# A hybrid block in float32: memory keys and values and the SSD half of the output projection between the stick-breaking heads, SSD products in runs, first stage in another order

## The reference

```python
proj = rmsnorm(h, norm_mix_g) @ w_in          # z, xbc, dt, q, k, v
xbc = silu(causal_dwconv(xbc, conv_w, conv_b))
y = ssd_chunked(xh, dt, a, bm, cm)            # 8 heads of 64, 4 chunks of 128 tokens
y_ssd = rmsnorm((y + d_skip * xh) * silu(z), ssd_norm_g)
# stick-breaking attention, 8 heads of 64: A[t,s] = sigmoid(z_ts) * prod_{s<j<t} (1 - sigmoid(z_tj)), s < t
y_sb = rmsnorm(stick_breaking_attention(q, k, v), sb_norm_g)
h = h + concat(y_ssd, y_sb) @ w_out
m = rmsnorm(mem, norm_mem_g)                  # 256 memory tokens
k = m @ w_xk; v = m @ w_xv                    # 4 heads of 128
q = rmsnorm(h, norm_xa_g) @ w_xq
h = h + softmax(q k^T / sqrt(128)) v @ w_xo
```

## Time and profile before

| | |
|---|---|
| time, median of 3 runs | 2195.87 us (2185.97 to 2202.16) |
| the profiled execution's own time | 2196.22 us |
| its span, first to last instruction | 2194.4 us |
| TensorE busy | 2087.9 us, 95% of the span |
| VectorE, ScalarE, GpSimd busy | 1061.4, 749.7, 229.7 us |
| mean granted TensorE clock | 0.96 |

### The profile page before, as it was taken

One profiled execution on the slowest core, in us unless ns is written; L12 is line 12 of the kernel. 1 busy time (PEld: TensorE's weight loads), 2 busy tenths in 40 slices (PEclk: granted clock), 3 DMA queues, 4 the chain that ended last, 5 costly groups with the idle time before them and its releaser, 6 DMA issues.

```text
span 2194.4 us, 28790 instructions
## 1 busy us (share of the span) xinstructions
PE 2087.9 (95%) x11578; PEld 1763.2 (80%) x11578; DVE 1061.4 (48%) x1429; ACT 749.7 (34%) x975; POOL 229.7 (10%) x198
## 2 busy tenths in 40 slices
PE   7998988999999999999899999999998899999997
PEld 5776656768888888898899999999886578888885
DVE  5654547454444454313244343435598634443434
ACT  4435653353223243331332222123434433222122
POOL 2001022020000022002320000002035210000001
PEclk9997789999999999899899999999999899999998
DMA  4213112212222222111122222222222022222221
GB/s 165 81 74 48 21 39 77 96 58 96 96 96 93 90 86 97 55 61 39 39 90 84 96 94 79 96 96 96 77 77 72 7 77 96 96 96 96 96 84 69
DMA packets 27792, 174.68 MB, mean 80 GB/s; under 512 B 4385, under 2 KB 4513, under 8 KB 7730
## 3 DMA queue, kind: packets, MB, share of 16 engines
q1 hardware_dynamic: 25680, 167.32, 21.5%
q0 software_dynamic: 1856, 5.90, 1.7%
q10 hardware_dynamic: 162, 0.10, 0.0%
HBM read 168.53 MB, written 4.78 MB: 79 GB/s over the span
## 4 chain that ended last, share of the span: by engine, by line
PE 69%; issue 18%; DVE 7%; ACT 4%; POOL 1%; DMA 0%; DVEq 0%; POOLq 0%; ACTq 0%
PE lin L425 56%; PE aux L1959 1%; ACT w_hi L359 1%; PE lin L1140 1%; DVE w_lo L366 1%; PE lin L1150 1%; PE aux L1528 1%; PE aux L1542 1%; POOL squares L601 1%; PE lin L1929 1%; PE aux L1943 1%; PE aux L1119 1%; PE aux L1120 1%; PE aux L1955 0%; PE aux L1556 0%
## 5 line engine op out<-in xcount | busy, mean ns | idle before, releaser
L425 PE MATMUL lin<-v_hi,w_hi 128*128 128x264 f32 (+1 forms) x1712 | 573.7, 335 | 4.8 <-DVE v_lo L586 3.4
L425 PE MATMUL lin<-v_hi,w_lo 128*128 128x264 f32 (+1 forms) x1712 | 571.1, 334 | 0.0
L425 PE MATMUL lin<-v_lo,w_hi 128*128 128x264 f32 (+1 forms) x1712 | 569.5, 333 | 0.0
L425 PE MATMUL lin<-x_hi,w_hi 128*128 128x512 f32 (+1 forms) x1224 | 436.2, 356 | 29.2 <-DMA cst<-in_consts 13.4
L425 PE MATMUL lin<-x_hi,w_lo 128*128 128x512 f32 (+1 forms) x1224 | 433.0, 354 | 0.0
L425 PE MATMUL lin<-x_lo,w_hi 128*128 128x512 f32 (+1 forms) x1224 | 432.6, 353 | 0.0
L366 DVE TENSOR_TENSOR w_lo<-w_raw,w_hi 128x2048 fp32r<-128x2048 f32 (+1 forms) x144 | 328.7, 2282 | 195.9 <-ACT w_hi L359 195.8
L359 ACT ACTIVATE w_hi<-w_raw 128x2048 fp32r<-128x2048 f32 (+1 forms) x155 | 292.9, 1890 | 289.9 <-PE lin L425 285.4
L425 PEld LDWEIGHTS lin<-v_hi,w_hi 128*128 128x128 f32 x1712 | 324.5, 190 | 39.6 <-DVE v_lo L586 3.8
L425 PEld LDWEIGHTS lin<-v_lo,w_hi 128*128 128x128 f32 x1712 | 324.4, 189 | 33.7 <-issue 0.7
L425 PEld LDWEIGHTS lin<-v_hi,w_lo 128*128 128x128 f32 x1712 | 324.3, 189 | 32.1
(11 more groups left out here) (341 smaller groups left out, 2358.9 us busy)
## 6 DMA issues: line engine op xcount, KB each, us to landing
w_raw<-in_weights SPq DMA_DIRECT2D x155, 1024.0 KB, 4.8
rel_by_distance<-rel_vec POOLq DMA_DIRECT2D x1, 2620.0 KB, 56.0
rel_bias<-rel_by_distance POOLq DMA_DIRECT2D x8, 264.0 KB, 3.0
h<-in_x_t SPq DMA_DIRECT2D x4, 512.0 KB, 8.2
out_t<-h SPq DMA_DIRECT2D x4, 512.0 KB, 2.8
mem_in<-in_mem_t POOLq DMA_DIRECT2D x1, 1024.0 KB, 5.1
cst<-in_consts SPq DMA_DIRECT2D x1, 512.0 KB, 9.8
col<-in_cols ACTq DMA_DIRECT2D x1, 67.0 KB, 6.0
```

The source lines that it names most:

```text
L425: last = nc.tensor.matmul(o, a, b, start=(k % (L.kc // k_banks) == 0 and p == 0), stop=((k + 1) % (L.kc // k_banks) == 0 and p == 2))
```

## The change

- **Order of units**: after V come xk, xv, then w_out in two halves, `w_out_a` (the SSD rows) and `w_out_b` (the stick-breaking rows), 2 units each, then xq. xk, xv and w_out_a no longer go through `pe_linear` and its slots.
- **Heads**: TensorE runs two **fills** in each head, one between the logits of the next head and the exponents, one after the values: in heads 0 and 1 the memory keys, in 2 and 3 the memory values, in 4 to 7 two output tiles of w_out_a each; the SSD norm's sums follow head 2. They go to two banks, `fill_banks`; ScalarE or VectorE empties them. The third bank of the exponents moves to `aux[:, 2, 256:512]`, beside the logits' third bank: the logits of head hd therefore wait for `w_att` of head hd - 2, ScalarE makes a copy `z_relu` of this bank's logits, and VectorE reads that.
- **Splits**: ScalarE makes w_hi of six units in the heads, GpSimd makes their w_lo (`pool_stick`), with the squares of the two mixer norms between them.
- **Head 0 earlier**: its logits, hi and lo parts and log terms stand in V; so do the sums and root of the memory norm, whose squares stand in K. The memory is loaded after the convolution's sums. Its operands lie in x_hi[4:8] and x_lo[4:8], its scale by token in `scale_tok[:, 1]`.
- **Bias table**: its columns are copied at the start, its write to DRAM starts when q and k are scaled.
- **SSD products**: `pe_ssd_back` issues the eight seg products in a row, then the eight state products; that of chunk 3 comes after V's second tile instead of the fourth.
- **First unit**: no wait for the constants, both output tiles at once in three passes (w_hi x_hi, w_lo x_hi, w_hi x_lo), with the semaphores of x_hi and x_lo; ScalarE's squares of the first norm come behind the split of unit 1, and VectorE adds them (`dve_squares`).
- **After the heads**: only w_out_b's 8 tiles (12 matmuls each), the root of `l_sb`, then xq.

The diff, cut to its core (buffer places and copied or deleted lines of the old order are left out):

```diff
...
-    ("w_out", 4, 8, 2, S1, False),
-    ("xk", 2, 8, 2, MEM, False), ("xv", 2, 8, 2, MEM, True), ("xq", 2, 8, 2, S1, False),
+    ("xk", 2, 8, 0, MEM, False), ("xv", 2, 8, 0, MEM, True), ("w_out_a", 2, 4, 0, S1, False),
+    ("w_out_b", 2, 4, 4, S1, False), ("xq", 2, 8, 2, S1, False),
...
+        def pe_first_unit(pe, L, hi, lo, N):
+            w = [t[:, 0, :].rearrange("p (k n) -> p k n", k=L.kc) for t in (w_hi, w_lo)]
+            pe.wait_ge(sem("w_hi_ready"), 1)
+            for p, (wp, xp_) in enumerate(((w[0], hi), (w[1], hi), (w[0], lo))):
+                if p == 1:
+                    pe.wait_ge(sem("w_lo_ready"), 1)
+                for m in range(L.tpu):
+                    for k in range(L.kc):
+                        if p == 0 and m == 0:
+                            pe.wait_ge(sem("operand_hi"), N.tiles0 + k + 1)
+                        elif p == 2 and m == 0:
+                            N.wait_operand(pe, k)
...
             act_evacuate(act, XBC, ...
-                after={(1, 1): lambda: act_root(act, l_mix)})
+                after={(0, 0): all_squares, (1, 1): lambda: act_root(act, l_mix)})
...
             next_lo(dve, XBC, 0, 0)
+            dve_squares(dve, l_mix)
             next_lo(dve, XBC, 1, 0)
...
+            dve_ssd_out(dve, 3)
+            dve_sb_lo(dve, 0)
             next_lo(dve, V, 1, 0)
-            dve_ssd_out(dve, 3)
+            dve_sb_lo(dve, 1)
+            dve_root(dve, l_mem)
...
-            pe_linear(pe, V, x_hi, x_lo, after={(0, 3): lambda: pe_ssd_back(pe, 3)})
+            pe_linear(pe, V, x_hi, x_lo, after={(0, 1): lambda: pe_memory_sums(pe),
+                                                (1, 1): lambda: pe_sb_first(pe)})
...
             for e in range(8):
-                g, o = e // 4, aux[...]
-                nc.tensor.matmul(o, xdt[:, e, :], seg[:, e, :], start=True, stop=(c == 0))
-                if c:
-                    r = slice(64 * g, 64 * g + 64)
-                    nc.tensor.matmul(o, state[r, e % 4, :], c_dec[r, e % 4, :], start=False, stop=True)
+                nc.tensor.matmul(out_of(e), xdt[:, e, :], seg[:, e, :], start=(e % 4 < 2),
+                                 stop=(c == 0 and e % 4 >= 2), skip_group_check=True)
+            if c:
+                for e in (0, 1, 4, 5, 2, 3, 6, 7):
+                    r = slice(64 * (e // 4), 64 * (e // 4) + 64)
+                    nc.tensor.matmul(out_of(e), state[r, e % 4, :], c_dec[r, e % 4, :], start=False,
+                                     stop=(e % 4 >= 2), skip_group_check=True)
...
+        z_relu = tmp[:, 2, 0:256]
+        fill_banks = [aux[:, 3, :], lin[1][:, 0, :]]
+        XK_FILL, XV_FILL, SUM_FILL, WA_FILL, FILLS = (0, 1), (2, 4), 3, 5, 13
+        def sb_logits(pe, hd):
+            pe.wait_ge(sem("sb_lo"), hd + 1)
+            if hd:
+                pe.wait_ge(sem("sb_stay"), hd)
+            if hd >= 2:
+                pe.wait_ge(sem("sb_w_raw"), hd - 1)
...
+            def mixed(t):
+                w, o = weights_of(WA.unit0 + t // 4, 4), bank(WA_FILL + t)
+                for k in range(4):
+                    if t == 0:
+                        l_ssd.wait_operand(pe, k)
+                    for r, (wp, xp_) in enumerate(((w[0], x_hi), (w[0], x_lo), (w[1], x_hi))):
+                        mm = nc.tensor.matmul(o, wp[:, k, t % 4 * P:t % 4 * P + P], xp_[:, k, 0:S1],
+                                              start=(k == 0 and r == 0), stop=(k == 3 and r == 2))
+                mm.then_inc(sem("fill_done"), 1)
+            for hd in range(2):
+                sb_logits(pe, hd + 1)
+                if hd == 0:
+                    wait_taken(pe, V)
+                memory_keys(hd, 0)
+                exponents(hd)
+                if hd:
+                    values(hd - 1)
+                memory_keys(hd, 1)
+            for hd in (2, 3):
+                sb_logits(pe, hd + 1)
+                memory_values(hd - 2, 0)
+                exponents(hd)
+                values(hd - 1)
+                memory_values(hd - 2, 1)
+                if hd == 2:
+                    ssd_sums()
+            for hd in (4, 5, 6):
+                sb_logits(pe, hd + 1)
+                mixed(2 * hd - 8)
+                exponents(hd)
+                values(hd - 1)
+                mixed(2 * hd - 7)
+            mixed(6)
+            exponents(7)
+            values(6)
+            mixed(7)
+            values(7)
...
+            def next_unit(hd):
+                if hd == 0:
+                    split_hi(act, XK.unit0 + 1, 0, V.tiles_end)
+                elif hd < 5 or hd == 6:
+                    unit, done = {1: (XV.unit0, 1), 2: (XV.unit0 + 1, 2), 3: (WA.unit0, 3), 4: (WA.unit0 + 1, 5),
+                                  6: (WB.unit0, 9)}[hd]
+                    act.wait_ge(sem("fill_done"), done)
+                    split_hi(act, unit, 0, 0)
...
+            for t in range(KD):
+                act_operand_hi(act, l_mem, t)
+            stay_high(0)
+            for hd in range(8):
+                if hd < 7:
+                    act_sb_log(act, hd + 1)
+                next_unit(hd)
+                if hd < 7:
+                    stay_high(hd + 1)
+                if hd < 6:
+                    act_sb_hi(act, hd + 2)
+                if hd == 0:
+                    act.wait_ge(sem("y_gated"), 4)
+                if hd < 2:
+                    for t in (2 * hd, 2 * hd + 1):
+                        act_operand(act, l_ssd, t, t % 2)
+                if hd == 2:
+                    act.wait_ge(sem("scale_ready"), l_mem.idx + 1)
+                    act.wait_ge(sem("operand_lo"), l_ssd.tiles0 + l_ssd.k)
+                weights_made(hd)
+                if hd in (2, 3):
+                    memory_values(hd - 2)
+                if hd == 2:
+                    ssd_root()
+                if hd in (4, 5, 6):
+                    output(hd - 4)
+            output(3)
...
             for hd in range(8):
                 if hd < 7:
                     stays(hd + 1)
+                    stay_low(hd + 1)
+                if hd < 6:
+                    dve_sb_lo(dve, hd + 2)
                 if hd < 2:
                     for t in (2 * hd, 2 * hd + 1):
                         dve_operand(dve, l_ssd, t)
+                if hd >= 4:
+                    mixed(2 * hd - 8)
                 dve.wait_ge(sem("sb_w_raw"), hd + 1)
                 masked(w_att).then_inc(sem("sb_w"), 1)
...
+            clear(l_ssd, l_mix.idx + 1)
+            pool.wait_ge(sem("w_lo_ready"), XK.unit0 + 1)
+            split_lo(pool, XK.unit0 + 1, 0, nc.gpsimd)
+            add_square(l_ssd, 0)
+            add_square(l_ssd, 1)
+            split_lo(pool, XV.unit0, 0, nc.gpsimd)
...
+            act_residual(act, WB, l_xa, after=lambda: act_root(act, l_sb))
...
+            dve_residual(dve, WB, N=l_xa, after=lambda: dve_root(dve, l_sb), scale=scale_d[:, 0:S1])
...
+            pe_linear(pe, WB, x_hi[:, 4:8, :], x_lo[:, 4:8, :], ready=lambda k: l_sb.wait_operand(pe, k),
+                      after={(0, 0): lambda: pe_squares(pe, l_sb)})
...
```

More of the change, by code:

```diff
@@ L432, in unit @@
                     do_at(after, 2 * i + j, m)
-            for_units(pe, L, unit, ready is not None or after is not None)
+            if first_unit:
+                for u in range(first_unit, L.units):
+                    unit(u % 2, u // 2)
+            else:
+                for_units(pe, L, unit, ready is not None or after is not None)
         def act_evacuate(act, L, tile, after=None):
@@ L601, in pool_squares, with dve_squares @@
                     nc.gpsimd.tensor_tensor(acc, acc, tmp[:, s, 0:N.n], ALU.add).then_inc(sem("square_added"), 1)
+        def dve_squares(dve, N):
+            for t in range(N.k):
+                dve.wait_ge(sem("square_added"), N.added0 + t)
+                dve.wait_ge(sem("square"), N.squares0 + t + 1)
+                acc = squares[:, N.slots[0], N.first:N.first + N.n]
+                nc.vector.tensor_tensor(acc, acc, tmp[:, t % 2, 0:N.n], ALU.add).then_inc(sem("square_added"), 1)
         TOKEN_SUMS = 300
@@ L1153, in values, with weights_of @@
                 mm.then_inc(sem("sb_pv"), 1)
-            pe.wait_ge(sem("ssd_state"), CHUNKS)
-            logits(0)
-            wait_taken(pe, V)
-            for hd in range(9):
-                if hd < 7:
-                    logits(hd + 1)
-                if hd < 8:
-                    exponents(hd)
+            def weights_of(unit, kc):
+                pe.wait_ge(sem("w_lo_ready"), unit + 1)
+                return [t[:, unit % 2, :].rearrange("p (k n) -> p k n", k=kc) for t in (w_hi, w_lo)]
@@ new lines, in memory_values @@
+            def memory_values(u, m):
+                w, o = weights_of(XV.unit0 + u, 8), bank(XV_FILL[u])[:, m * 256:m * 256 + 256]
+                for k in range(KD):
+                    for q, (wp, xp_) in enumerate(((w[0], x_hi), (w[0], x_lo), (w[1], x_hi))):
```

(15 more changed lines are left out.)

308 lines of the change are left out of this document (184 added, 124 removed).

## The result

The kernel after takes 2161.5 us, median of four runs (2158.0 to 2162.9), beside 2196.0 before (2186.0 to 2202.2, four runs): ratio 0.9855, 95% interval 0.9812 to 0.9898. Run again on another occasion it took 2161.3 against 2191.8, ratio 0.9849 (0.9821 to 0.9876). The prediction was 2163.7, range 2140 to 2190. By the threshold of the forecast, 1% of the time, that is faster; it stays under 2%. The profiled execution has a span of 2159.8 us, 34.6 under the 2194.4 of before.

A forecast was written before the change was run, and what follows sets the result against it. TensorE, busy 95% of the span, was taken as the bound, so its own time counts. From 2196.2 us: -2.5 - 6.8 + 12.8 + 10 + 8 - 54 = -32.5, giving 2163.7 us, range 2140 to 2190.

The forecast's parts named there:

- A: First unit: weight split ahead of the squares lets TensorE's second unit start earlier; gain 2.5 us, bounds nothing to 5.
- B: SSD products in runs avoid alternating 128 and 64 rows; 3.4 us saved in each of chunks 1 and 2, together 6.8.
- Chunk 3: SSD product placed two V tiles earlier: no gain of its own, TensorE waits some 3.3 us for VectorE's last matrix.
- C: Heads at full speed with two fills each, 16.4 us a head: 137.5 us from the end of V, 12.8 more than before.
- The two waits: Heads 0 and 1: two SSD operands in ScalarE's queue make TensorE wait 4.5 and 2 us.
- E: Six w_lo splits on GpSimd beside the heads hold up VectorE: 8 us lost, bounds nothing to 15.
- D: Half speed in the heads: 23 us of it at 0.43 lost per microsecond, 10 us lost; bounds nothing to 28.
- F: From the heads to xq: 88.6 us before becomes 34.5, a change of -54 us, bounds -48 and -58.
- the clock would stay as now: Rival for the heads: half speed for 0.52 of the time, since being busy does not suffice; 2186 us, chance 0.16.
- the spell of 37 us: Half speed from 192 to 229 us in the kernel before, begun with some 7 us without work; read as short gaps keeping it low.

The follow-up runs named there:

- the fastest kernel: Kernel after with GpSimd's six w_lo splits moved to VectorE and w_raw made ahead of the SSD operands in heads 0 and 1: 2140.7 us, ratio 0.976.
- VectorE's splits: Kernel after with all six w_lo splits on VectorE behind each head's sb_lo instead of on GpSimd: 2149.5 us, ratio 0.979.
- thin: Kernel after with GpSimd's six w_lo splits computing 16 of 2048 columns: 2147.9 us, ratio 0.979.
- the kernel with filled waits: Kernel after with 56 extra matmuls ahead of logits(2) and 14 ahead of logits(3), in TensorE's waits: 2157.3 us, ratio 0.983.

## Why the prediction was right, and where its terms were not

- **The page.** The clock line reads 7 in slices 4 and 5 only, and 8 in slice 6; nothing in the sum hangs on it.
- **A**, 2.5 predicted, 2.8 measured; the unit waits as forecast for ScalarE's evacuation behind the squares.
- **B**, 6.8 predicted, 8.3 measured. The cause was right; the state products take 0.60 us, under the bound of 0.9 to 2. I had set it by the eight products of 128 rows, 0.92. Why eight of 64 rows take less was not tried; the order of their quadrants makes no difference.
- **Chunk 3**, a wait of 3.3 predicted, 3.4 measured. V ended 10.9 earlier, 9.3 predicted. That half speed can follow this wait, as in ten of twelve profiles, is in no term.
- **C** without its waits was 137.5 - 6.5 = 131.0 from the end of V. In the fastest kernel it is 135.6 (177.6 to 313.2), less its wait of 1.7 and 2.5 for 6 us at half speed: 131.4. The head of 16.4 is 16.3. The two waits were put at 4.5 and 2.0; taking their cause away gives 6.8.
- **E** was 8, range 0 to 15; measured 11.0 (VectorE's splits) to 11.5 (thin). The worse of the two ways came, the cut into the masks, in each head that has a split. I had taken the middle between 0.9 and 2.6 a head; the earlier trace rows spoke for the upper end.
- **D** is the term that the runs take apart. Half speed for 28 us (granted clock 0.91 from the end of V) was near the 23 taken. But a price of 0.43 us for each, added to the waits, counts twice: the kernel with filled waits got back 0.5 for 6 us, and taking E's and C's delays away took 20 of the 26 us at half speed with them. Waits, splits and half speed were 6.5 + 8 + 10 = 24.5 together; the runs show 19.2 for the two delays with the clock that hangs on them, and 4.2 that remain: 23.4. That the sum came so close is in part luck: its terms were wrong in both directions, E too small and D, as a term of its own, too large.
- **F**, 54 predicted, 54.4 measured: root 9.6 us after the heads (9.7), tiles 3.3 apart, last operand 39.2 (38.4), xq at 34.2 (33.5, and 1 more for its sums, which would fall behind xq's first matmul).
- **The rivals.** That the clock would stay as now, "being busy does not suffice", had 0.16. Its premise holds, as the heads without fills show: 94% busy at a clock of 0.57. The forecast's reading of the spell of 37 us, that short gaps keep the clock low, doesn't: it stood at 0.50 through 15 us of it without a gap. What the rival missed is that fills differ from the heads' own matmuls; the argument against it on record, that they are "the dense kind that ran at 1.00", was the one that decided. How much it decides I had not seen: without them the change would have lost its gain in the heads, at 99 to 114 us of half speed.

Open: which property of the heads' own matmuls (64-row and 64-column tiles, short ones, their order) lets the clock sink, and why the heads without fills take longer here than the 124.7 us of before (some 146 from the end of V even without the two delays); ScalarE and VectorE have more to do in them, but that was not tried apart.

## What to carry over

Put independent, dense matmuls between the steps of a stage whose TensorE clock is low: here 43 us of them shortened the stretch instead of lengthening it. Before placing a product earlier, see that its operand is ready: two V tiles earlier chunk 3's products waited 3.4 us, with half speed behind the wait in ten of twelve profiles; whether the later place would make after faster was not tried. Before moving elementwise work onto GpSimd, look at what VectorE does in those microseconds; if that is on the chain, even short instructions with two SBUF inputs can wait the whole GpSimd instruction out (0.29 us became 4.67), and the same work cost less on VectorE itself. Price waits and half speed together, by a run of the stage, not as a sum: where another engine's chain sets the pace, speed lost by TensorE costs little.

## What was unexpected of the hardware

- A change between 128-row and 64-row matmuls costs 0.30 to 0.31 us; eight 64x64 products of 128 columns in a run take 0.60.
- With 18.8 of 20.0 us busy TensorE kept a clock of 0.57, and 0.50 through 16 us without any gap; with 16.3 of 16.3, fills among them, it had 1.00.
- A wait of 3.4 us ahead of dense matmuls left the clock at 1.00 in two profiles and at half speed for 3.4 to 9.3 us in ten, with the same program up to there in nine of them.
- One GpSimd subtraction of 4.6 us gets in between VectorE's masks of 0.29 each every time and holds them until it has ended, 5.3 us for four.
